# Two attention layers and a mixer block in one kernel: later norm weights, x turned between products, one product ahead of the last turned tile

## What is computed

```
shift, scale, gate = split(silu(c) @ w_ada + b_ada, 3)       # c_ctx for the context rows
h = x * (1.0 + scale) + shift
(a_q, a_i, a_ff, a_fb, b_q, b_k, b_v, c_q, ..., g_lat) = split(h @ w_in)
y_a = hgrn2_mixer(a_q, a_i, a_ff, a_fb, ...)                 # two scans, rms_norm with hg_norm_g
q, k = rope(rms_norm(b_q, ga_qn)), rope(rms_norm(b_k, ga_kn))
y_b, y_c, y_d = attention over b, c (differential, df_lambda, df_subln_g), d (windowed, wn_sink)
y = concat([y_a, y_b, y_c, y_d]) * silu(g_lat)
x_new = layer_norm(alpha * x + gate * (y @ w_out), ln_g, ln_b)
```

## Time and profile before

| | us |
|---|---|
| median of 3 runs (lowest, highest) | 2242.8 (2241.7, 2244.02) |
| profiled execution | 2239.02 |
| its span | 2237.2 |
| mean granted TensorE clock | 0.963 |
| PE busy | 2033.1 |
| DVE busy | 1138.0 |
| ACT busy | 755.6 |

### The profile page before, as it was taken

One profiled execution on the slowest core, in us unless ns is written; L12 is line 12 of the kernel. 1 busy time (PEld: TensorE's weight loads), 2 busy tenths in 40 slices (PEclk: granted clock), 3 DMA queues, 4 the chain that ended last, 5 costly groups with the idle time before them and its releaser, 6 DMA issues.

```text
span 2237.2 us, 26204 instructions
## 1 busy us (share of the span) xinstructions
PE 2033.1 (91%) x9904; PEld 1376.3 (62%) x9904; DVE 1138.0 (51%) x2482; ACT 755.6 (34%) x1621; POOL 54.1 (2%) x96
## 2 busy tenths in 40 slices
PE   4989999899779899898888798999899997999999
PEld 1465565455444455564455446885688886887887
DVE  2555136555663856317466567996544435333333
ACT  2133123555441113223464323336422324222322
POOL 2000000000010000000000020000000000000000
PEclk8999999999889999999899898998999998999999
DMA  9111010002362211111000242321133331333331
GB/s 288 29 57 38 24 62 22 17 1 62 127 227 43 76 47 38 38 48 57 20 1 9 87 98 57 92 79 30 54 92 100 94 96 57 102 95 94 95 94 66
DMA packets 152684, 157.27 MB, mean 70 GB/s; under 512 B 5676, under 2 KB 114384, under 8 KB 152560
## 3 DMA queue, kind: packets, MB, share of 16 engines
q1 hardware_dynamic: 146672, 137.91, 20.2%
q0 software_dynamic: 5888, 17.68, 2.8%
HBM read 151.37 MB, written 4.19 MB: 70 GB/s over the span
## 4 chain that ended last, share of the span: by engine, by line
PE 72%; DVE 17%; ACT 6%; issue 3%; DMA 1%; POOL 0%; ACTq 0%; SPq 0%; DVEq 0%; POOLq 0%
PE psum L750 16%; PE psum L1204 9%; PE psum L1205 9%; PE psum L1206 9%; PE psum L934 5%; PE psum L778 5%; PE psum L762 4%; DVE stats L2032 3%; PE psum L967 3%; PE psum L948 2%; PE psum L713 2%; ACT arena L1485 2%; DVE arena L2296 2%; PE psum L796 1%; ACT arena L1311 1%
## 5 line engine op out<-in xcount | busy, mean ns | idle before, releaser
L750 PE MATMUL psum<-arena 128*128 128x512 f32 (+1 forms) x1280 | 460.2, 516 | 0.8 <-ACTq L1314 0.8
L1311 ACT ACTIVATE arena<-psum 128x256 f32<-128x256 f32 (+6 forms) x520 | 205.3, 422 | 694.7 <-PE psum L713 212.9
L1204 PE MATMUL psum<-part,part 128*128 128x512 f32 x992 | 390.8, 394 | 14.8 <-DVE part L2415 7.0
L1205 PE MATMUL psum<-part,part 128*128 128x512 f32 x992 | 390.0, 393 | 0.0
L1206 PE MATMUL psum<-part,part 128*128 128x512 f32 x992 | 389.8, 393 | 0.0
L750 PEld LDWEIGHTS psum<-arena 128*128 128x128 f32 x1280 | 240.2, 191 | 195.9 <-issue 179.5
L2411 DVE TENSOR_TENSOR part<-arena,part 128x1024 fp32r<-128x1024 f32 x112 | 137.1, 1226 | 251.9 <-ACT part L1311 251.9
L1311 ACT ACTIVATE part<-arena 128x1024 fp32r<-128x1024 f32 (+1 forms) x198 | 174.2, 913 | 219.5 <-PE psum L1206 149.8
L1204 PEld LDWEIGHTS psum<-part,part 128*128 128x128 f32 x992 | 188.3, 190 | 57.1 <-issue 13.9
L2032 DVE TENSOR_REDUCE stats<-psum 128x1 f32<-128x768 f32 (+6 forms) x208 | 138.8, 709 | 153.9 <-PE psum L934 152.5
L1205 PEld LDWEIGHTS psum<-part,part 128*128 128x128 f32 x992 | 188.6, 190 | 39.8
(11 more groups left out here) (269 smaller groups left out, 2005.7 us busy)
## 6 DMA issues: line engine op xcount, KB each, us to landing
arena<-in_w_in SPq DMA_DIRECT2D x75, 512.0 KB, 4.2
arena<-in_w_mlp SPq DMA_DIRECT2D x64, 512.0 KB, 3.9
arena<-in_w_ada SPq DMA_DIRECT2D x48, 512.0 KB, 5.6
arena<-in_w_gate SPq DMA_DIRECT2D x32, 512.0 KB, 4.0
arena<-in_w_out SPq DMA_DIRECT2D x24, 512.0 KB, 3.7
arena<-in_w_in SPq DMA_DIRECT2D x16, 256.0 KB, 3.2
arena<-in_w_branch SPq DMA_DIRECT2D x8, 512.0 KB, 4.9
arena<-in_x POOLq DMA_DIRECT2D x4, 512.0 KB, 9.1
```

What stands on the lines that cost most here:

```text
L750: mm = pe.matmul(bank(b)[:, c0:c1], lhs[:, k, m * P:(m + 1) * P], ring.view(tag, l, k // 2)[:, k % 2, c0:c1], start=k == 0, stop=k == kt - 1)
L1204: pe.matmul(dst, lo, x_hi_, start=first, stop=False)
L1205: pe.matmul(dst, hi, x_lo_, start=False, stop=False)
L1311: return act.activation(dst, src, ACT.Copy)
```

## The change

Three things move; no arithmetic changes. In `pool_program` a wait for the turn of the last modulation row of layer 0 stands ahead of `load_gains(0)`. On PE, ACT and DVE only tiles 0 and 1 of x are turned and modulated ahead of `layer(0)`; tiles 2 to 5 come one at a time ahead of the products b of tiles 0 to 3. On PE the wait for z of tile 5 and its turn move from the end of `layer_end(0)` to behind the first product b of layer 1; ACT's and DVE's order there is unchanged.

```
@@ tensor_program
             def modulate(l, m, x_tile):
+                if l == 0:
+                    pe.wait_ge(*x_loads[m].at(m))
                 for half in range(2):
...
                         if n == 1 and m >= 1 and l < DEPTH - 1:
                             pe.wait_ge(*tail_dve.at("z", l, m - 1))
                             modulate(l + 1, m - 1, z[:, m - 1, :])
-                if l < DEPTH - 1:
-                    pe.wait_ge(*tail_dve.at("z", l, last_q - 1))
-                    modulate(l + 1, last_q - 1, z[:, last_q - 1, :])
 
             def layer(l):
                 for t in range(2):
                     beside = stream(l, t)
-                    for _ in range(AHEAD):
+                    for m in range(AHEAD):
+                        if t == 0 and l == 0 and m + 2 < TT:
+                            modulate(0, m + 2, stage_x[m + 2])
                         next(beside)
+                        if t == 0 and l > 0 and m == 0:
+                            pe.wait_ge(*tail_dve.at("z", l - 1, TT - 1))
+                            modulate(l, TT - 1, z[:, TT - 1, :])
                     scan_inputs(l, t)
...
             run(ada([(0, n) for n in range(4)]))
-            for m in range(TT):
-                pe.wait_ge(*x_loads[m].at(m))
+            for m in range(2):
                 modulate(0, m, stage_x[m])
             layer(0)
@@ scalar_program, and the same in vector_program
-                    for _ in range(AHEAD):
+                    for m in range(AHEAD):
+                        if t == 0 and l == 0 and m + 2 < TT:
+                            modulate(0, m + 2)
                         next(beside)
...
-            for m in range(TT):
+            for m in range(2):
                 modulate(0, m)
@@ pool_program
             for m in range(TT):
                 fetch(m)
+            pool.wait_ge(*turn_done.at("ada", 0, 3))
             load_gains(0)
```

## The result

| | before | after |
|---|---|---|
| median, us (lowest to highest, runs) | 2242.25 (2240.93 to 2244.02, 4) | 2223.1 (2222.2 to 2228.11, 4) |
| ratio to before | 1 | 0.9919, 95% interval 0.9905 to 0.9933 |
| profiled execution | 2239.02 | 2222.2 |
| its span | 2237.2 | 2220.3 |
| mean granted clock | 0.963 | 0.968 |

What follows compares the result with a forecast made beforehand. PE, busy 91% of the span, was taken to bound the kernel, so only its idle or slow places count: 8.0 + 1.0 + 8.5 = 17.5 us off the profiled 2239.0 gives 2221.5, as a median 2225.3; range 2220 to 2233.

Steps and rivals of the forecast that it cites:

- Part 1: Layer 0 start: gains issued behind the last modulation row let w_ada end earlier, 8.0 us saved, bounds 6.0 and 8.7.
- The gains' landing: Layer 0 start: the late gains, which DVE waits for, all land at 51.5 us, bounds 47.8 and 59.2.
- Their cover: Layer 0 start: the gains could land 1 to 2.6 us later than 51.5 without delaying PE.
- Part 2: Before the scan's inputs: turning x between products removes three PE waits of 0.33 us, 1.0 us saved, bounds 0 and 1.6.
- three turns of 1.07 between them: First products of layer 0: three key turns of 1.07 us add 3.2 us before tile 3's keys are turned at 86.1.
- Part 3: End of layer 0: layer 1's first product fills PE's 7.03 us gap, 8.5 us saved, bounds 7.0 and 8.9.
- Gains cost only their bytes: Rival at w_ada: something else slows the engines, gains cost 0.9 us, saving only 10.4 in sum, 2232.4 us; chance 0.12.
- The late-gains rival: Layer 0 start: gains land at 59.2, DVE holds PE 6 us, saving 11.5 in sum, 2231.3 us; chance 0.13.
- the prediction's rule (G - 53.3): Layer 0 start: gains landing at time G cost nothing up to 53.3 us; each us later costs one.
- The slower rival: Layer 0 start: DVE's wait for gains outweighs everything gained, from a landing at 75.3 us, time 2247.3; chance 0.03.
- late weights: Layer 1's first product: its weights or bank come late, the saving there falls to 1 or 2 us, 2232 to 2233; chance 0.05.
- PE carrying both shifts to the end: Rest of the kernel: no later stage sets a time of its own, so the 17.5 us saved reach the end.

Runs made afterwards that it cites:

- the repetition of the changed kernel: The changed kernel run again unaltered, on the same chip as the version with early constants and late x: 2226.54 us, ratio 0.9931.
- the own-row experiment: The kernel before, its ten early gains transfers reading 128 different rows of w_in instead of one row 128 times: 2234.28 us, ratio 0.9973.
- the later-gains run: The changed kernel, with POOL waiting for the first product b instead of the last modulation row before issuing the gains: 2232.11 us, ratio 0.9954.
- the doubling: The kernel before, with every gains transfer of layer 0 issued a second time, early, into an unused stretch: 2251.24 us, ratio 1.0032.
- the removal: The kernel before with only the gains issued late, behind the last modulation row: 2231.84 us, ratio 0.9955.
- each of two edits alone: The changed kernel with tiles 3 to 5 of x behind w_ada: 2222.77 us; or with PE's first operands ahead of the other constants: 2224.23 us.
- both edits: The changed kernel with early constants and tiles 3 to 5 of x behind w_ada: 2219.94 us first, 2220.34 us in its repetition.

## Why the prediction was right

- **The time.** 2225.3 was forecast, 2223.1 came, within the range of 2220 to 2233; 17.5 us were forecast in sum, and the changed kernel's trace shows 7.5 + 1.6 + 8.6 = 17.7 in place. The misses of parts 1 and 2 (0.5 too much, 0.6 too little) cancel, which is luck. So is part of the agreement at the end: the lead of the profiled execution is 9.1 us at the scan's inputs, 11.0 at the turn of tile 4 (761.49 against 750.51), 19.9 at the last attention and 16.9 at the end, and in the repetition of the changed kernel that came 15.7 us below, the turn of tile 4 starts 3.5 us later (753.97), where its scan's inputs were 0.4 later.
- **Part 1** was put at 8.0 with bounds of 6.0 and 8.7; it gave 7.5. The weights ran at 386 GB/s and not the 394 assumed, which explains 0.3 of the 0.5 us. PE's wait shrank to 1.46 us and not to some 3. PE did work at its slow rate until about 26 us, against "clock 1.00 or short at 0.50", but the last blocks wait for DMA, so it cost nothing that the trace shows. Its lower bound, the share of q0, was sound: the own-row experiment shows the same stretch without it.
- **The gains' landing** was put at 51.5; it was 50.4. The working (6.0 us of work beside weights) held, with q0 taking 40.2% of 38 to 51 us, 5.2 us; other executions of kernels with late gains show 49.9 to 52.2. Their cover was put at 1 to 2.6 us beyond that; it was 3.8 at the keys and, by the later-gains run, 4.4 at tile 4's turn (DVE ended tile 2's modulation at 52.2, PE needed it at 56.6). What was too careful was the row of gaps between DVE's head rows: they ran at 7.73 us a tile with the modulation, not 7.9.
- **Part 2** was put at 1.0 with a bound of 1.6; it was 1.56. The three waits of 0.33 went as stated. The step that failed is "three turns of 1.07 between them": a turn between products costs 0.87.
- **Part 3** was put at 8.5; it was 8.6. The step by step order held, up to DVE's head rows ending it: PE waits 0.56 us for the last one, as DVE had become what is late next. The clock at 1.00 in the former gap was as foreseen.
- **The rivals.** "Gains cost only their bytes" is refuted by the doubling and by the removal; but what the Trainium skill says of small descriptors (DMA: Bandwidth & Descriptors, "Why small descriptors are slow (HBM only)") is not refuted, though the prediction took it to be. With separate addresses the ten transfers cost 1.1 us by the rows, near the 1 us or a little more that the prediction estimated from the page. (The page's 27% is 3 cycles of 11, so 38% over the beats and not 27; with it, 32 bytes of metadata on 256 and 394 GB/s the estimate is 1.3 us.) The prediction's sentence that the trace disagrees with that size put down to the size what came with the repeated row. The late-gains rival did not occur. The later-gains run puts its price at 7.0 us for G = 60.2, where the prediction's rule (G - 53.3) gives 6.9; the match is luck in part, since the wait was 5.3 us, at the turn of tile 4 and not at the keys, and the slow clock behind it, which the rule leaves out, added the rest. The slower rival and late weights did not occur.
- **"PE carrying both shifts to the end"** did not hold exactly: the changed kernel's profiled execution lost 3 us of it in its last 670, behind gaps that the change does not touch, and a repetition of the same kernel did not.

## What to carry to other kernels

A transfer that spreads one row over 128 partitions can hold the DMA engines far longer than its bytes say; put it where nobody needs the engines, or look for the stretch in which the engines are busy and the GB/s low. When a load is moved earlier or later, ask for the two limits apart, the bytes ahead of the last block and the moment at which the consumer starts to free the ring: here each of two edits alone gave 0.8 us and nothing, and the two together 2.9 to 3.7 us. A wait for data of another engine is cheapest behind one piece of work that needs none of it, if the engine that delivers can follow: DVE's queue, not PE's, decided how much of the gap was won.

## What the runs showed of the hardware

- Ten transfers that each read one row of HBM 128 times (eight of 256 bytes, one of 16 and one of 512) cost the 16 engines 6.0 us for 0.34 MB; as many pieces from 128 different rows of w_in cost 1.1 us. A second such set beside the first cost 8.4 us more.
- PE's clock fell to 1.2 GHz in or behind idle gaps of 5.3, 7.0 and 7.4 us. With shorter gaps the same place differs between executions: with both edits it fell for about 7 us (0.50 from 22 to 28) behind a gap of 2.06 us in the first run, and stayed at 2.4 behind one of 1.88 us in the repetition; w_ada's last block came at 32.14 and 32.27 all the same. Behind one of 2.67 us it stayed at 2.4 in the kernel before, and in two executions of the changed kernel it was low for 6.2 us and for 2.8 of the next 10. Such differences in the last 670 us add up to 3.5 us of time in a program that is the same.
- Eight transposes take 1.04 to 1.06 us from the start of the first to the end of the last, but a product that follows at once starts 0.87 us behind their start.
